# Behind the scan: low parts written over the weight panels, four high parts kept, splits three panels ahead, a shorter repair, later statistics

## The reference, cut to what matters

```python
def first_block(x, c, ...):
    mod = (silu(c) @ w_mod + b_mod)[:, None, :]
    sh1, sc1, g1, sh2, sc2, g2 = jnp.split(mod, 6, axis=-1)
    h = rms_norm(x) * (1.0 + sc1) + sh1
    u, v, z, xbc, dt_raw, gate_a, gate_b = jnp.split(h @ w_in, offs, axis=-1)
    y_a = sgu_branch(u, v, ...)                 # gelu, norm, causal 128x128 products
    y_b = ssd_branch(z, xbc, dt_raw, ...)       # conv, chunked scan, gated group norm
    mixed = sigmoid(gate_a) * (y_a @ w_branch_gm) + sigmoid(gate_b) * (y_b @ w_branch_ssm)
    x = x + g1 * (mixed @ w_out)
    h2 = rms_norm(x) * (1.0 + sc2) + sh2
    x = x + g2 * (square(relu(h2 @ w_ff1)) @ w_ff2)
    return rms_norm(x, final_norm_w)

def second_block(x, ...):                       # layer i = 0: attention, i = 1: pool mixer
    for i in range(2):
        x = layer_norm(ALPHA * x + 0.5 * swiglu(x, w_gu[i, 0], w_down[i, 0]), ...)
        y = moba_attention(x, ...) if i == 0 else pool_mixer(x, ...)
        x = layer_norm(ALPHA * x + y, ...)
        x = layer_norm(ALPHA * x + 0.5 * swiglu(x, w_gu[i, 1], w_down[i, 1]), ...)
    return x
```

## Time and profile before

| | us |
|---|---|
| median of 3 runs | 1521.05 (1519.83 to 1527.03) |
| profiled execution, its own time | 1525.12 |
| its span, first to last instruction | 1522.8 |
| PE busy | 1475.5 |
| DVE busy | 1114.7 |
| ACT busy | 839.3 |
| POOL busy | 184.6 |

### The profile page before, as it was taken

How to read it: one execution, slowest core, us unless ns; L and a number is a source line. 1 busy time by engine, 2 the same in 40 slices (tenths; PEclk the granted TensorE clock), 3 DMA queues, 4 the chain that set the end, 5 groups by cost and what they waited for, 6 DMA issues and landing times.

```text
span 1522.8 us, 25731 instructions
## 1 busy us (share of the span) xinstructions
PE 1475.5 (97%) x10189; PEld 1365.3 (90%) x10189; DVE 1114.7 (73%) x1474; ACT 839.3 (55%) x1135; POOL 184.6 (12%) x169
## 2 busy tenths in 40 slices
PE   8999998999999999999989989999999999899997
PEld 7999998889888899888989988889888898888887
DVE  7788987887877758666586697665966659886655
ACT  5655567655555446555454565554665545565543
POOL 0120003562000010000130020001300013030001
PEclk9999999999999999999999999999999999999999
DMA  8957756646445654555534335555455553445550
GB/s 328 370 212 277 262 203 228 216 150 215 191 173 202 239 219 169 191 193 193 193 132 176 137 119 213 193 194 192 146 202 196 186 186 136 152 182 195 191 194 28
DMA packets 43401, 295.94 MB, mean 194 GB/s; under 512 B 5052, under 2 KB 7228, under 8 KB 8750
## 3 DMA queue, kind: packets, MB, share of 16 engines
q1 hardware_dynamic: 40574, 280.24, 50.7%
q0 software_dynamic: 2736, 14.41, 2.7%
HBM read 291.44 MB, written 3.19 MB: 193 GB/s over the span
## 4 chain that ended last, share of the span: by engine, by line
PE 55%; DVE 7%; ACT 2%; issue 1%; DMA 0%; ACTq 0%; DVEq 0%
PE banks L708 24%; PE banks L710 12%; PE banks L723 5%; PE banks L725 4%; PE banks L726 4%; DVE w_lo L1868 2%; DVE part L1963 1%; ACT w_hi L1298 1%; DVE pw L2612 0%; DVE XS L2122 0%; PE banks L795 0%; PE banks L794 0%; PE banks L796 0%; DVE XS L1945 0%; PE banks L1205 0%
## 5 line engine op out<-in xcount | busy, mean ns | idle before, releaser
L1868 DVE TENSOR_TENSOR w_lo<-raw,w_hi 128x1024 fp32r<-128x1024 f32 x490 | 613.0, 1270 | 279.4 <-ACT w_hi L1298 275.4
L1298 ACT ACTIVATE w_hi<-raw 128x1024 fp32r<-128x1024 f32 x490 | 508.6, 1055 | 366.1 <-PE banks L710 176.9
L708 PE MATMUL banks<-H,w_hi 128*128 128x512 f32 x1504 | 522.2, 392 | 1.9 <-DVE w_lo L1868 1.9
L710 PE MATMUL banks<-H,w_lo 128*128 128x256 f32 x1504 | 420.4, 280 | 0.0
L708 PEld LDWEIGHTS banks<-H,w_hi 128*128 128x128 f32 x1504 | 282.3, 188 | 64.9 <-DVE w_lo L1868 2.8
L710 PEld LDWEIGHTS banks<-H,w_lo 128*128 128x128 f32 x1504 | 282.4, 188 | 0.0
L708 PE MATMUL banks<-HH,w_hi 128*128 128x512 f32 x480 | 166.8, 392 | 1.8 <-DVE w_lo L1868 1.8
L891 PE MATMUL banks<-H,w_lo 128*128 128x256 f32 x512 | 146.2, 286 | 2.0 <-ACT gate_a L1538 2.0
L893 PE MATMUL banks<-H,w_hi 128*128 128x256 f32 x512 | 144.1, 282 | 0.0
L894 PE MATMUL banks<-H,w_hi 128*128 128x256 f32 x512 | 144.1, 281 | 0.0
L723 PE MATMUL banks<-HH,w_lo 128*128 128x256 f32 x480 | 134.3, 280 | 0.0
(11 more groups left out here) (369 smaller groups left out, 2605.4 us busy)
## 6 DMA issues: line engine op xcount, KB each, us to landing
raw<-in_panels SPq DMA_DIRECT2D x265, 1024.0 KB, 4.8
rows<-cum_rows POOLq DMA_DIRECT2D x16, 384.0 KB, 4.6
late_w<-in_panels POOLq DMA_DIRECT2D x4, 1024.0 KB, 5.1
bias_rows<-rev POOLq DMA_DIRECT2D x1, 2048.0 KB, 11.4
XS<-in_x_t SPq DMA_DIRECT2D x4, 256.0 KB, 5.3
near<-bias_rows POOLq DMA_DIRECT2D x8, 128.0 KB, 3.4
out_t<-XS SPq DMA_DIRECT2D x4, 256.0 KB, 2.6
ws<-in_ws_t POOLq DMA_DIRECT2D x1, 512.0 KB, 11.3
```

Of the source, the lines that this page charges most:

```text
L708: pe.matmul(bank, w_hi[:, panel_slot, at:at + P], operand[:, kk, :, :].rearrange("p a t -> p (a t)"), start=starts and c == chunks[0], sto ...
L710: return pe.matmul(bank[:, 0:T], w_lo[:, panel_slot, at:at + P], operand[:, kk, 0, :], start=False, stop=stops and c == chunks[-1])
L1298: act.activation(w_hi[:, sl, w], raw[:, r, w], ACT.Copy).then_inc(panel_hi, 1)
L1868: vec.tensor_tensor(w_lo[:, sl, w], raw[:, r, w], w_hi[:, sl, w], ALU.subtract).then_inc(panel_lo, 1)
```

## The change

1. From stage out on (`DEEP`), the low part of a panel is written over the panel itself (`deep_lo` lies over `raw`), and the high part into one of 4 slots (`deep_hi` lies over `w_hi` and `w_lo`). ACT's split waits only for the panel to have landed (the first four also for the old slots to be free). SP's load of panel q + 4 waits until PE has used both halves of panel q.
2. At borders, both halves of F and F + 1 are split ahead of the last group's post work. In the first group of the next stage the splits of F + 2 and F + 3 stand in other places; the mean is subtracted in two halves, the second between the 4th and 5th scaled block.
3. The repair: DVE multiplies the 4 banks by root in one instruction, ACT makes the 4 shift blocks (mean times root times edge, plus bias), DVE adds them in one instruction. The Silu that follows is the ordinary one of 2 blocks. ACT splits the first half of F + 4 ahead of its part of this.
4. The statistics stand behind block k = 2, 3 or 4 of the unscaled group (`STATS_BEHIND`), and the additions into `part` are ordered anew; in att_out all stand behind the post work.
5. In ff2, the four late modulation panels are worked one per two panels.
6. In the attention stages the value copies wait for `half_used` of their own panel.

The diff, cut to what the prediction speaks of:

```diff
+DEEP = len(DENSE)
+HI_SLOT = {(DEEP + i) % RAW: i // SPLIT * SPLIT + (DEEP + i) % SPLIT for i in range(RAW)}
...
 EDGE = 2
+STATS_BEHIND = {"out": 3, "ff2": 2, "down0": 2, "att_out": 4, "down1": 2, "pool_out": 3}
...
+        deep = ExitStack()
+        deep_lo = sb("deep_lo", [P, RAW, PANEL], F32R, deep)
+        deep_hi = sb("deep_hi", [P, RAW, PANEL], F32R, deep)
+        deep.close()
...
-                    last = kind in URGENT and isinstance(g, int) and g == n - 1
-                    if last and STAGES[s][0] in NORMED:
-                        take_up(s, g, (FIRST_GROUP[s] + u) % 2)
-                    elif last:
-                        split(*ahead(s, g, u, turn, 1), halves=(0,))
-                        take_up(s, g, (FIRST_GROUP[s] + u) % 2)
-                        split(*ahead(s, g, u, turn, 1), halves=(1,))
-                    else:
-                        split(*ahead(s, g, u, turn, 1))
-                        take_up(s, g, (FIRST_GROUP[s] + u) % 2)
+                    split(*ahead(s, g, u, turn, 1))
...
-                sp.wait_ge(panel_lo, 2 * (RAW * n + r - RAW - MODS + 1))
+                sp.wait_ge(half_used, 2 * (RAW * n + r - RAW - MODS + 1))
                 sp.dma_start(raw[:, r, :], panels[RAW * n + r]).then_inc(loaded[r], 16)
...
-                        last.then_inc(half_used, 1)
-                        if p == 0 and half == 0:
-                            whole_stats(stage)
+                                if b == BANKS - 1 and c % 2:
+                                    last.then_inc(half_used, 1)
+                            if k == STATS_BEHIND[stage]:
+                                whole_stats(stage)
...
-                    need(act, half_used, 2 * (q - SPLIT if behind is None else behind) + half + 1)
+                    if sl < DEEP:
+                        need(act, half_used, 2 * (q - SPLIT) + half + 1)
+                    elif isinstance(q, int) and q < DEEP + RAW:
+                        act.wait_ge(half_used, 2 * (DEEP - SPLIT + (q - DEEP) % SPLIT) + half + 1)
                     w = slice(half * PANEL // 2, (half + 1) * PANEL // 2)
-                    act.activation(w_hi[:, sl, w], raw[:, r, w], ACT.Copy).then_inc(panel_hi, 1)
+                    act.activation(high(sl)[:, w], raw[:, r, w], ACT.Copy).then_inc(panel_hi, 1)
+
...
+                    if stage_name in CENTRED:
+                        act.wait_ge(S["edges_kept"], edges_count(stage_name))
+                        for b in range(BANKS):
+                            act.activation(ev[:, 1 - G, b, :], st[:, 3, :], ACT.Identity, bias=edges[:, b, 1:2],
+                                           scale=edges[:, b, 0:1]).then_inc(S["shift_ready"], 1)
+                    rest(s, G, lambda: split_half(q + SPLIT, 1))
                 return post

-            def first_biased(dest, a):
-                def rest(s, G, next_half):
-                    act.wait_ge(S["first_scaled"], UNSCALED_ORDER.index(BEFORE_STAGE[STAGES[s][0]]) + 1)
-                    for b in range(BANKS):
-                        act.activation(dest(G)[:, b, :], dest(G)[:, b, :], ACT.Identity, bias=edges[:, b, a:a + 1])\
-                            .then_inc(S["first_kept"], 1)
-                    next_half(0)
-                    next_half(1)
-                    if STAGES[s][3] == "relu2":
-                        round_into(HH)(s, 0, G)
...
+                act.wait_ge(S["first_scaled"], UNSCALED_ORDER.index(BEFORE_STAGE[STAGES[s][0]]) + 1)
+                act.activation(ev[:, G, 0:2, :], ev[:, G, 0:2, :], ACT.Silu).then_inc(activated, 1)
+                next_half()
+                round_into(HH, 2)(s, 0, G)
...
-                alone = name in SUMMED_AHEAD
-                adds = {3: (5, 6)} if alone else {0: (1, 2), 1: (3,), 2: (4, 5), 3: (6,)} if name == "att_out" else \
-                    {1: (4,), 2: (5,), 3: (6,)}
+                early = name in ("out", "pool_out")
                 for b in range(BANKS):
                     bank_post(INDEX[name], g, G, b, new_x)
-                    if b == BANKS - 1:
+                    if early and b:
+                        add_block(name, BANKS + b - 1)
                         unscaled_lo(name, BANKS + b - 1)
-                        if alone:
-                            vec.wait_ge(S["norm_part"], BANKS * SUMMED_AHEAD.index(name) + BANKS)
-                    for m in adds.get(b, ()):
+                    elif b:
+                        unscaled_lo(name, BANKS + b - 1)
+                if name == "att_out":
+                    for m in (1, 2, 3, 4):
                         add_block(name, m)
-                    if 0 < b < BANKS - 1:
-                        unscaled_lo(name, BANKS + b - 1)
+                elif not early:
+                    vec.wait_ge(S["norm_part"], BANKS * SUMMED_AHEAD.index(name) + BANKS)
+                if not early:
+                    add_block(name, 5)
+                    add_block(name, 6)
                 add_block(name, KD - 1)
-                split_after(split, name, 0)
                 unscaled_lo(name, KD - 1)
...
+                def away(g):
+                    vec.tensor_tensor(by_group(xb)[:, g, :, :], by_group(xb)[:, g, :, :],
+                                      st[:, 0, :].unsqueeze(1).to_broadcast([P, BANKS, T]), ALU.add).then_inc(S["norm_centred"], BANKS)
+
                 def post(s, G):
                     q, b = FIRST_PANEL[s] + SPLIT, stat_bank(stage_name)
...
                                                       ALU.subtract))
                         vec.tensor_scalar(st[:, 1, :], st[:, 1, :], LN_EPS, None, ALU.max).then_inc(S["stat_var"], 1)
-                    split_after(split, stage_name, 1)
+                    if stage_name == "att_out":
+                        split_half(q, 0)
                     if mean:
                         vec.wait_ge(S["mean_kept"], [n for n in UNSCALED_ORDER if n in CENTRED].index(stage_name) + 1)
-                        away = st[:, 0, :].unsqueeze(1).to_broadcast([P, BANKS, T])
-                        for g in range(2):
-                            vec.tensor_tensor(by_group(xb)[:, g, :, :], by_group(xb)[:, g, :, :], away, ALU.add)\
-                                .then_inc(S["norm_centred"], BANKS)
+                        away(0)
                     vec.wait_ge(S["stat_root"], n + 1)
-                    scaled(0)
-                    for m in range(KD):
-                        if m + 1 < KD:
-                            scaled(m + 1)
...
-                        first = qk[:, 0:BANKS, :] if STAGES[s][3] == "keep" else ev[:, G, :, :]
+                    for m in range(KD + 1):
+                        if m == BANKS and mean:
+                            away(1)
+                        if m < KD:
+                            scaled(m)
+                        if m:
+                            lo(m - 1)
+                        if m in (2, 4, 6):
+                            split_half(*{2: (q, 1), 4: (q + 1, 0), 6: (q + 1, 1)}[m])
+                    if mean:
+                        vec.tensor_tensor(st[:, 3, :], st[:, 0, :], st[:, 2, :], ALU.mult)
+                    first = qk[:, 0:BANKS, :] if STAGES[s][3] == "keep" else ev[:, G, :, :]
                     root = st[:, 2, :].unsqueeze(1).to_broadcast([P, BANKS, T])
                     products_done(s, 0)
                     if stage_name != "ff2":
                         vec.tensor_copy(edges[:, :, :], banks[:, BANKS * G:BANKS * G + BANKS, T:T + EDGE])\
                             .then_inc(S["edges_kept"], 1)
+                    vec.tensor_tensor(first, group_banks(G), root, ALU.mult).then_inc(taken, 1)
+                    split_half(q + SPLIT, 0)
+                    vec.wait_ge(taken, FIRST_GROUP[s] + 1)
                     if mean:
-                        vec.wait_ge(S["edges_kept"], [n for n in UNSCALED_ORDER if n != "ff2"].index(stage_name) + 1)
-                        for b in range(BANKS):
-                            last = vec.scalar_tensor_tensor(first[:, b, :], st[:, 0, :], edges[:, b, 0:1],
-                                                            banks[:, BANKS * G + b, 0:T], ALU.mult, ALU.add)
-                        last.then_inc(taken, 1)
-                        vec.wait_ge(taken, FIRST_GROUP[s] + 1)
-                        vec.tensor_tensor(first, first, root, ALU.mult).then_inc(S["first_scaled"], 1)
...
-                late = q - SPLIT - FIRST_PANEL[INDEX["ff2"]] - 1
-                if 0 <= late < LATE:
-                    mod_panel(MODS_IN_GATES + late)
+                late = q - SPLIT - FIRST_PANEL[INDEX["ff2"]]
+                if 0 <= late < 2 * LATE and late % 2 == 0:
+                    mod_panel(MODS_IN_GATES + late // 2)
...
-            split_half(att_half(12)[0] + SPLIT, 0)
-            split_half(att_half(12)[0] + SPLIT, 1)
             for b in range(BANKS):
                 unscaled_lo("att_out", b)
+            for half in range(2):
```

(1 more changed line is left out.)

217 lines of the change are left out of this document (85 added, 132 removed).

## The result

The changed kernel takes 1504.97 us (median of 4 runs, 1503.96 to 1509.66), the kernel before 1520.44 beside it (1519.05 to 1527.03): ratio 0.990, 95% interval 0.987 to 0.993. The forecast was 1502.5, in 1495 to 1510. Measured again beside three variants it took 1506.27 against 1521.48, ratio 0.990 (0.988 to 0.992).

What follows compares the result with a forecast made beforehand. PE, busy 1475.5 of 1522.8 us, was taken as the bound, with border waits and half clock to win. Terms summed to 18.5: 1525.1 to 1506.6 for the profiled execution, 4.1 above the median, so 1502.5, range 1495 to 1510.

Steps and rivals of the forecast that it cites:

- The bound, and the worth of borders: PE is busy 1475.5 of 1522.8 us; four long border waits cost their length and some 10 us more at half clock.
- out to ff1: Border out to ff1: PE waits 0.7 instead of 3.44 for `part`, at full clock; gain 5.4, less 0.3, so 5.1 us.
- Modulation panels: In ff2, one late modulation panel per two panels fits DVE's time, so PE's 1.8 wait for `w_lo` goes; gain 2.0 us.
- down0 to qk: Border down0 to qk: the 4.54 wait before group 2 and its half clock go; gain 4.5 + 1.7 + 0.3 = 6.5 us.
- att_out to gu1: Border att_out to gu1: bound by DVE's chain; gain 0.2, less 1.7 for one half-clock stretch, net -1.5 us.
- down1 to gu2: Border down1 to gu2: statistics waits of 0.2 + 0.2 and 1.7 for `w_lo` go; gain 2.1, or 1.1 if margin missed.
- pool_out to gu3: Border pool_out to gu3: gain 5.7, less a new 2.2 wait for F + 4's second half, net 3.5 us; other end 2.9.
- C: Rival, all panel loads: they come late once landing exceeds 14.6 us; at 15.5 the time is 1542; chance 0.03.
- the 9.8 us of cover: Panel loads: landing may take up to 14.6 us against a median of 4.8, so later loading costs 0.
- A: Rival, borders out and pool_out: splits ahead of the posts delay `part`, half clock returns; gain some 10, 1511; chance 0.17.
- D: Rival, every border: the norm and repair chain takes the gain back one group later; gain 6 to 7, 1515; chance 0.07.
- the statistics term: Later statistics points cut PE's waits for `part`: 0.7 for 3.44 at out, 2.7 for 4.55 at att_out, 0.2 at pool_out.

Runs made afterwards that it cites:

- three variants: Changed kernel with F + 4's second half split earlier; that plus F + 5's first half; that plus F + 1's second half behind att_out's additions: 1505.99, 1506.42, 1503.25 us.
- the run with the modulation panels: Changed kernel with ff2's four late modulation panels again worked one per panel: 1507.72 us, ratio 0.992 to the kernel before.
- the gate run: Changed kernel, but ACT's split of panel q again waits until PE has used the same half of q - 2: 1550.34 us, ratio 1.018 to the kernel before.

## Why the prediction was right, and where it was off

*The bound, and the worth of borders.* Right: nothing changed in mid stage (gu0 and down0, 172.4 both), and nearly everything came from the places where PE had waited and its clock behind them. The total was 2.4 us less than worked out (16.1 for 18.5), most of it in ff1 and at gu2 and gu3. At gu1 the number is right by luck.

*out to ff1.* Right: 5.4 worked out, 5.7 measured, with a wait of 0.48 for 0.7 and the half clock gone. But I took off 0.3 for F + 4 and later. PE does not wait for F + 4 there, but 1.20 for F + 6, and it costs 1.8: ff1 and ff2 behind group 0 take 168.9, and 167.1 in the four traces without such a wait. That is a term that was mis-sized: 1.8 and not 0.3. F + 6's split stands on DVE behind the post work of group 1, which I had not looked at.

*Modulation panels.* 2.0 worked out, 2.1 by its own run. In the table it is hidden (0.3 for 1.7), since the 1.8 just named falls in the same stretch.

*down0 to qk.* The size is right (7.3 for 7.0, attention taken in), half of the reason is not. I gave the gain to ACT's split that stands ahead of the shifts; with that alone undone 0.3 came back, and with the old repair besides 4.8. What was wrong was where the chain of the earlier trace rows is cut: ACT's four operations no longer follow DVE's five ahead of the splits of F + 4, but run beside DVE's. The new place of the split beside the old repair was not run.

*att_out to gu1.* Right: bound by DVE, `part` later than before relative to PE, and a wait of 2.51 for 2.7. Net +1.4 for +1.5, but that is luck. I had the second half of F + 4 no later than before and charged 1.7 for half clock behind its wait, and behind that wait the clock stayed at 1.00 (894.60). The half clock came at the statistics instead. What it took from PE's own products there cost nothing, since PE waited another 2.40 for F + 4 afterwards; it only made that wait shorter than 4.5. In place of the 1.7 stands the chain of DVE, 894.85 - 869.73 = 25.1 instead of 23.7. That is the step that was wrong. From the first unscaled product PE now gets to the second half of F + 4 after 35.0 us, against 33.9 before. About 0.7 of the excess is the statistics' own products at half clock: DVE's variance (L2123) starts 2.2 us behind their start here, and 1.4 in the run with the modulation panels, where the half clock began 0.9 behind their start.

*down1 to gu2.* 1.2 for 2.1: the wait for `w_lo` did not go but fell from 1.7 to 1.0. I had said that it costs 1 if the thin margin is missed; it was.

*pool_out to gu3.* 2.4 for 3.5. PE's part is right (group 0 5.2 shorter; I had 5.7); the chain was 1330.91 - 1307.57 = 23.3 instead of 22.7, and the other wait 2.41 instead of 2.2. DVE's idle time in the repair accounts for more than that, and its first piece ends with ACT's shifts, which stand behind a table load of 1.28 (what they would do ahead of it was not run). DVE, then ACT:

```profile
888.13 1.22 DVE L1862 TENSOR_TENSOR deep_lo<-raw,deep_hi 128x1024 fp32r<-128x1024 f32 x1
890.70 1.23 DVE L2154 TENSOR_TENSOR ev<-ev 128x1024 f32<-128x1024 f32 x1 [1.35 <-ACT ev L1436]
892.62 0.69 DVE L2169 SCALAR_TENSOR_TENSOR ev<-ev 128x512 f32<-128x512 f32 x1 [0.70 <-ACT ev L1453]
893.57 1.23 DVE L1862 TENSOR_TENSOR deep_lo<-raw,deep_hi 128x1024 fp32r<-128x1024 f32 x1 [0.26 <-ACT deep_hi L1300]
```

```profile
887.12 1.28 ACT L1379 ACT_TABLE_LOAD   x1
888.53 2.07 ACT L1436 ACTIVATE ev<-st,edges 128x256 f32<-128x256 f32 x4
```

(These are gu1's; in gu3 the wait for the shifts is 1.35 as well.) I had counted fewer waits for ACT here, not new ones.

*The rivals.* C did not come about, but its working was wrong: loads one panel later cost nothing in mid stage and 47.7 us at the borders, so the 9.8 us of cover do not hold there. (By its own sum the excess at 15.1 is 0.5 and not 0.4, 24 us and not 19.) Had the load been issued one panel later, the sum would have said 1502 and the chip 1553. A named the right danger (in-order engines, splits ahead of the posts); where such a split has to wait, the gate run shows the price, 45 us. D is what half of the statistics term did: 10.4 of 16.5 us are given back.
